# A branch that is not taken, between two quads of experts instead of behind the last

## The chip, the cores and the metric

The kernel runs on one core of a Trainium2 chip. The metric is the device time of one execution in microseconds (us), as the median of the runs. Five engines have a program each: TensorE (PE), VectorE (DVE), ScalarE (ACT), GpSimd (POOL) and SyncE (SP), which here only starts DMA transfers. They meet through semaphores.

## The reference, cut to what matters

Two layers over 256 tokens of width 1024, all in float32. In each layer comes attention of one kind or another, and then a mixture of experts in 4 groups of 8. A token picks one group, and in it two experts:

```python
for l in range(DEPTH):                                   # 2
    mod = c_act @ mod_w[l] + mod_b[l]
    ...
    x = x + gate1 * mix                                  # attention
    h = rms_norm(x, norm2_g[l]) * (1.0 + scale2) + shift2
    x = x + gate2 * hier_moe(h, ...)
# hier_moe, for each group g of 4, each expert e of 8:
hid = silu(hf @ w1[g, e]) * (hf @ w3[g, e])              # 1024 -> 512
y = y + (hid * gate[:, g, e]) @ w2[g, e]                 # 512 -> 1024
```

The weights of the 32 experts of a layer are read from memory whole: 3 x 2 MB each, 192 MB a layer.

## The kernel before

**Experts by quads.** The 32 experts are worked on as `QUADS` = 8 quads of four. An expert has 32 seats; the tokens that chose it are numbered (`m.rank`), and those with numbers 1 to 32 sit in the first round. For a quad, TensorE gathers the seated tokens of four experts by products with a 0/1 matrix `m.sel` (L772), VectorE and ScalarE scale and shift them into `m.seated` (L1538 and L953, the helper that records every activation), TensorE makes the two hidden products with four experts side by side (L788, four blocks of 32 products), VectorE multiplies them (L1542), TensorE turns the result (L800), makes the output products (L813, two blocks), VectorE applies the gate of the residual (L1549), and TensorE spreads the rows back over the tokens and adds them to banks 4 to 7 (L823). At the end of a quad VectorE makes `m.sel` for the next one (L1524); at its start it makes `m.sel_gate` (L1533). On each engine the eight quads are one hardware loop (`Fori`).

**Weights by a ring.** Every weight passes through `m.ring`, six slots of 2 MB (one unit each). A quad is 12 units, two to a block of L788 or L813. SP issues the units in the order of use (L323 for dense weights, L335 for experts) and waits before each until `m.ring_used`, which TensorE raises as it finishes a unit, has freed its slot. The next layer's dense units follow the eighth quad in the same ring. Its first four are the modulation weights, called F0 to F3 here: TensorE multiplies F0, F1 and F2 (L511), then turns the normed tokens (L540), then multiplies F3.

**Further rounds.** More than 32 tokens may choose an expert. The routing counts them and writes a row of flags, `m.over_i` (semaphore `over_ready`); flag 1 says that some expert has more than 32. Behind the loop over the quads each of PE, ACT, DVE and SP loads the flag into a register and branches:

```python
        pe.wait_ge(s["over_ready"], l + 1)
        with pe.If(pe.value_load(m.over_i[0:1, 1:2]) > 0):
            with pe.Fori(1, ROUNDS) as r:
                with pe.Fori(0, QUADS) as quad:
```

The body is another copy of the quad's code, run seven times over all eight quads with the next 32 seats each time and its own semaphores (`m.moe[l, "more"]`), and with weights loaded again. With the flag at 0 it is jumped over. Behind it TensorE makes one small product into bank 7 (L846), which only signals `end`; VectorE then copies the four banks to `m.x` (L1566; in the last layer ScalarE copies two of them, L1176), and the norm of the next layer or the output transfer (L357) follows.

Of the kernel before, what the change touches and what calls it, by code (L numbers as in the profile page):

```python
# [87 lines left out]
LAYER_UNITS = DENSE_UNITS + QUAD_UNITS * QUADS  # L88
ATT = P + T
# [208 lines left out]
def program_sync(sp, m, a, out):  # L298
# [18 lines left out]
    for l in range(DEPTH):  # L317
# [13 lines left out]
        with sp.Fori(0, QUADS) as quad:  # L331
            for u in range(QUAD_UNITS):
                g = g0 + u
                sp.wait_ge(m.ring_used, g - RING + 1 + QUAD_UNITS * quad)
                sp.dma_start(slot_pair(m, slot_of(g)), expert_unit(m, a, l, quad, u)).then_inc(  # L335
                    m.ring_full[slot_of(g)], 16)

        s = m.moe[l, "more"]
        sp.wait_ge(m.s["over_ready"], l + 1)
        with sp.If(sp.value_load(m.over_i[0:1, 1:2]) > 0):  # L340
            sp.wait_ge(m.ring_used, g0 + QUAD_UNITS * QUADS)
            with sp.Fori(1, ROUNDS) as r:
                with sp.Fori(0, QUADS) as quad:
# [7 lines left out]
                    sp.sem_inc(s["quads"], 1)  # L351
    rows = out.rearrange("b (t p) d -> p (b t) d", p=P)
# [138 lines left out]
def program_tensor(pe, m):  # L491
# [334 lines left out]
    def experts(l):  # L826
# [4 lines left out]
        with pe.Fori(0, QUADS) as quad:  # L831
            def landed(u):
                pe.wait_ge(m.ring_full[slot_of(g0 + u)], fills(g0 + u) + 32 * quad)
            quad_of_experts(e, quad, quad + 1, [slot_of(g0 + u) for u in range(QUAD_UNITS)], landed, m.ring_used)
        e = m.moe[l, "more"]
        pe.wait_ge(s["over_ready"], l + 1)
        with pe.If(pe.value_load(m.over_i[0:1, 1:2]) > 0):
            with pe.Fori(1, ROUNDS) as r:
                with pe.Fori(0, QUADS) as quad:
# [5 lines left out]

        pe.matmul(bank[7][0:1, 0:P], m.above[:, 0:1], m.ident[:, :], start=False, stop=True,  # L846
                  skip_group_check=True).then_inc(m.moe[l, "end"], 1)
# [100 lines left out]
def program_scalar(act, m, a):  # L948
# [186 lines left out]
    def experts(l):  # L1135
        with act.Fori(0, QUADS) as quad:
            quad_of_experts(l, "first", quad)
        act.wait_ge(s["over_ready"], l + 1)
        with act.If(act.value_load(m.over_i[0:1, 1:2]) > 0):
            with act.Fori(1, ROUNDS) as r:  # L1140
                with act.Fori(0, QUADS) as quad:
                    quad_of_experts(l, "more", (r - 1) * QUADS + quad)

# [53 lines left out]
def program_vector(dve, m):  # L1197
# [355 lines left out]
    def experts(l):  # L1553
        dve.wait_ge(s["row_ready"], 4 * (l + 1))
        with dve.Fori(0, QUADS) as quad:
            quad_of_experts(l, "first", quad, quad, quad + 1, m.iota[:, 0:SEATS])
        with dve.If(dve.value_load(m.over_i[0:1, 1:2]) > 0):
            with dve.Fori(1, ROUNDS) as r:
                seats = m.iota[:, bass.ds(SEATS * r, SEATS)]
                seat_tokens(m.moe[l, "more"], slice(0, 4), seats)  # L1560
                with dve.Fori(0, QUADS) as quad:
                    quad_of_experts(l, "more", (r - 1) * QUADS + quad, quad, (r - 1) * (QUADS + 1) + quad + 1, seats)
        dve.wait_ge(m.moe[l, "end"], 1)
# [93 lines left out]
```

## Time and profile before

| | |
|---|---|
| median of 3 runs | 1378.91 us (1375.66 to 1379.0) |
| the profiled execution, its own time | 1371.47 us |
| its span, first to last instruction | 1369.7 us |
| TensorE busy | 989.0 us (72%) |
| VectorE busy | 262.8 us (19%) |
| ScalarE busy | 213.9 us (16%) |
| mean granted TensorE clock | 0.868 of full speed |
| DMA | 489.78 MB, mean 358 GB/s over the span |

The profile is of one execution; times in it are microseconds from its first instruction. "Busy" leaves out register loads, branches and waits, so that these show only as idle time of their engine, with "issue" as the releaser when nothing else is seen to end it. SPq is the instruction queue of SP, PEld the weight loads of TensorE.

### The profile page before, as it was taken

What the parts mean: (1) busy time and instruction counts of PE and PEld (TensorE: products, weight loads), DVE (VectorE), ACT (ScalarE), POOL (GpSimd) and SP (SyncE); (2) the same over time, 40 slices, a digit from 0 to 9 for tenths busy, and PEclk for the clock granted to TensorE, in tenths of its full rate; (3) what the DMA queues carried; (4) which work ended last, traced back from release to release, by engine and by line L of the source; (5) the groups of instructions that cost most, each with busy time, mean ns of one, the idle gap of its engine ahead of it and who ended that gap; (6) DMA issues with size and microseconds to landing.
All of it is one profiled execution on the core that took longest, in us unless ns stands there. A gap on an engine that the chain in (4) does not pass through costs nothing.

```text
span 1369.7 us, 13973 instructions
## 1 busy us (share of the span) xinstructions
PE 989.0 (72%) x5668; PEld 443.5 (32%) x5668; DVE 262.8 (19%) x573; ACT 213.9 (16%) x431; POOL 30.4 (2%) x89
## 2 busy tenths in 40 slices
PE   4999898667565766766679999967476675757665
PEld 1445555222121222222146665532121231212121
DVE  0545534101000010100020366410000010000101
ACT  2223314001000000100010353410000010000000
POOL 3000000000000000000000022000000000000000
PEclk9999999788887888888789999999887888878787
DMA  9973716999999999999999336569999999999995
GB/s 355 392 224 123 307 62 278 423 422 422 423 421 422 422 423 422 421 422 423 422 405 376 136 117 253 235 277 422 423 422 423 422 422 422 422 422 422 422 422 216
DMA packets 90826, 489.78 MB, mean 358 GB/s; under 512 B 18208, under 2 KB 18336, under 8 KB 37544
## 3 DMA queue, kind: packets, MB, share of 16 engines
q1 hardware_dynamic: 87776, 487.95, 87.4%
q10 hardware_dynamic: 3016, 1.37, 0.4%
q8 instruction: 22, 0.36, 0.1%
q14 instruction: 12, 0.10, 0.0%
HBM read 488.25 MB, written 1.05 MB: 357 GB/s over the span
## 4 chain that ended last, share of the span: by engine, by line
DMA 53%; PE 39%; DVE 4%; issue 1%; ACT 1%; SPq 1%; DVEq 0%
DMA ring<-in_moe_w_dram 52%; PE bank L546 8%; PE bank L788 7%; PE bank L813 7%; PE bank L586 4%; PE bank L699 4%; PE bank L511 2%; DMA ring<-in_mod_w_dram 1%; PE bank L638 1%; SPq L335 1%; PE bank L540 1%; PE bank L654 1%; PE bank L749 1%; PE bank L823 1%; DVE tmp L1404 0%
## 5 line engine op out<-in xcount | busy, mean ns | idle before, releaser
L788 PE MATMUL bank<-ring,region 128*32 128x512 f32 x2048 | 303.9, 748 | 189.2 <-DMA ring<-in_moe_w_dram 187.5
L813 PE MATMUL bank<-ring,region 128*32 128x512 f32 x1024 | 168.5, 818 | 122.9 <-DMA ring<-in_moe_w_dram 122.9
L788 PEld LDWEIGHTS bank<-ring,region 128*32 128x32 f32 x2048 | 83.6, 133 | 396.1 <-issue 394.4
L813 PEld LDWEIGHTS bank<-ring,region 128*32 128x32 f32 x1024 | 46.0, 143 | 232.7 <-issue 232.7
L546 PE MATMUL bank<-ring,hT 128*128 128x512 f32 x256 | 115.4, 602 | 2.7 <-ACT hT L953 2.7
L1542 DVE TENSOR_TENSOR region<-region,bank 128x512 f32<-128x512 f32 x16 | 11.0, 688 | 497.6 <-PE bank L788 497.6
L953 ACT ACTIVATE region<-bank,shift,scale 128x128 f32<-128x128 f32 x64 | 24.1, 457 | 353.2 <-PE bank L772 353.2
L1549 DVE TENSOR_TENSOR region<-bank,region 128x512 f32<-128x512 f32 x32 | 20.6, 686 | 281.1 <-PE bank L813 281.1
L823 PE MATMUL bank<-region 128*128 128x512 f32 x128 | 59.2, 605 | 13.4 <-DVE region L1549 13.4
L546 PEld LDWEIGHTS bank<-ring,hT 128*128 128x128 f32 x256 | 47.9, 193 | 59.4 <-issue 56.7
L511 PE MATMUL bank<-ring,c_wide 128*32 128x512 f32 x384 | 52.0, 670 | 18.0 <-DMA ring<-in_mod_w_dram 18.0
L772 PEld LDWEIGHTS bank<-region,h 128*128 128x128 f32 x512 | 59.5, 192 | 7.7 <-issue 6.7
L586 PE MATMUL bank<-hT,ring 128*128 128x256 f32 x256 | 59.4, 392 | 2.7 <-ACT hT L953 2.7
L772 PE MATMUL bank<-region,h 128*128 128x128 f32 x512 | 60.0, 275 | 0.8 <-DVE region L1524 0.8
L1132 ACT COPY region<-bank 128x256 f32<-128x256 f32 x16 | 6.0, 372 | 349.2 <-PE bank L800 349.2
L699 PE MATMUL bank<-ring,hT 128*128 128x512 f32 x128 | 57.3, 598 | 0.4 <-issue 0.3
L586 PEld LDWEIGHTS bank<-hT,ring 128*128 128x128 f32 x256 | 49.8, 197 | 11.6 <-ACT hT L953 2.7
L953 ACT ACT_TABLE_LOAD x34 | 43.6, 1283 | 4.3 <-issue 3.7
L823 PEld LDWEIGHTS bank<-region 128*128 128x128 f32 x128 | 23.0, 189 | 52.0 <-DVE region L1549 29.0
L1538 DVE TENSOR_SCALAR region<-bank,scale,shift 128x128 f32<-128x128 f32 x64 | 21.9, 404 | 57.0 <-PE bank L772 57.0
L420 POOL TENSOR_TENSOR pr<-pr,strict 128x384 f32<-128x384 f32 x16 | 18.1, 1129 | 659.9 <-ACT pr L953 659.9
L699 PEld LDWEIGHTS bank<-ring,hT 128*128 128x128 f32 x128 | 23.5, 190 | 26.7 <-issue 26.7
(217 smaller groups left out, 649.7 us busy)
## 6 DMA issues: line engine op xcount, KB each, us to landing
ring<-in_moe_w_dram SPq DMA_DIRECT2D x192, 2048.0 KB, 20.9
ring<-in_mod_w_dram SPq DMA_DIRECT2D x24, 2048.0 KB, 12.3
ring<-in_ev_w_in_dram SPq DMA_DIRECT2D x6, 2048.0 KB, 22.0
ring<-in_od_w_in_dram SPq DMA_DIRECT2D x6, 2048.0 KB, 19.2
ring<-in_ev_w_out_dram SPq DMA_DIRECT2D x2, 2048.0 KB, 7.6
ring<-in_od_w_out_dram SPq DMA_DIRECT2D x2, 2048.0 KB, 8.1
x<-in_x_dram ACTq DMA_DIRECT2D x1, 1024.0 KB, 5.1
out_dram<-x SPq DMA_DIRECT2D x4, 256.0 KB, 2.5
```

Of the source, the lines that this page charges most:

```text
L420: pool.tensor_tensor(m.pr[hh % 2][:, :], m.pr[hh % 2][:, :], m.strict[:, :], ALU.mult).then_inc(m.s["sb_masked"], 1)
L511: last = pe.matmul(out[32 * j:32 * j + 32, :], m.c_wide[:, k, :], w[:, k - rows * e, i * COL:(i + 1) * COL], start=first, stop=end, skip_g ...
L546: last = pe.matmul(bank[b][:, 0:cols], m.hT[:, k, t * P:(t + 1) * P], w[:, k, :], start=(k == 0), stop=(k == KC - 1))
L586: last = pe.matmul(bank[proj_bank(i)][:, c * T:(c + 1) * T], w[:, k, lo:lo + P], m.hT[:, k, :], start=(k == 0), stop=(k == KC - 1))
L699: last = pe.matmul(bank[out_bank(half, i)][:, :], m.hT[:, 4 * half + k, t * P:(t + 1) * P], w[:, k, u * COL:(u + 1) * COL], start=(k == 0) ...
L772: last = pe.matmul(bank[2 + k // 4][:, (k % 4) * P:(k % 4 + 1) * P], m.h[:, t, k * P:(k + 1) * P], m.sel[:, t, :], start=(t == 0), stop=(t ...
L788: last = pe.matmul(bank[which][32 * j:32 * j + 32, :], m.seated[:, 4 * part + k, 32 * j:32 * j + 32], w, start=(part == 0 and k == 0), sto ...
L813: last = pe.matmul(bank[half][32 * j:32 * j + 32, :], m.hidT[:, 2 * part + c, 32 * j:32 * j + 32], w, start=(part == 0 and c == 0), stop=( ...
L823: pe.matmul(bank[4 + 2 * half + t][:, :], m.back[:, t, :], m.y_seat[:, half * COL:(half + 1) * COL], start=False, stop=False, skip_group_c ...
L953: return act.activation(out, in_, f, **kw)
L1538: ts(m.seated[:, k, :], bank[2][:, k * P:(k + 1) * P], m.scale[:, k:k + 1], m.shift[:, k:k + 1], ALU.mult, ALU.add).then_inc(e["seated_dve ...
L1549: tt(m.y_seat[:, cols], bank[half][:, :], m.gate2[:, cols], ALU.mult).then_inc(e["y_copied"], 1)
```

## The change

On PE, ACT, DVE and SP the loop over eight quads is split into one over `FIRST_QUADS` = 6 and one over the last two, both with the same body, and the wait for `over_ready`, the load of the flag and the branch over the further rounds stand between the two. TensorE's closing product L846 stays behind the last quad. So each engine's program has one more copy of the quad's code in each layer. Inside the branch there are new waits, so that the tiles which the rounds share with the first round are free, and VectorE makes the seventh quad's `m.sel` again before it leaves the branch. GpSimd has no part in it.

```diff
@@ -86,6 +86,7 @@
 O_OUT_AT = (15, 14)
 QUAD_UNITS = 12
 LAYER_UNITS = DENSE_UNITS + QUAD_UNITS * QUADS
+FIRST_QUADS = QUADS - 2
 ATT = P + T
 SCALE = HD ** -0.5
 EPS = 1e-6
@@ -328,17 +329,21 @@
                     load_mod_cols(sp, m, a, layer, group, m.got["late_cols"])
                 router_loads(sp, m, a)
         g0 += DENSE_UNITS
-        with sp.Fori(0, QUADS) as quad:
+
+        def quad_loads(quad):
             for u in range(QUAD_UNITS):
                 g = g0 + u
                 sp.wait_ge(m.ring_used, g - RING + 1 + QUAD_UNITS * quad)
                 sp.dma_start(slot_pair(m, slot_of(g)), expert_unit(m, a, l, quad, u)).then_inc(
                     m.ring_full[slot_of(g)], 16)
 
+        with sp.Fori(0, FIRST_QUADS) as quad:
+            quad_loads(quad)
+
         s = m.moe[l, "more"]
         sp.wait_ge(m.s["over_ready"], l + 1)
         with sp.If(sp.value_load(m.over_i[0:1, 1:2]) > 0):
-            sp.wait_ge(m.ring_used, g0 + QUAD_UNITS * QUADS)
+            sp.wait_ge(m.ring_used, g0 + QUAD_UNITS * FIRST_QUADS)
             with sp.Fori(1, ROUNDS) as r:
                 with sp.Fori(0, QUADS) as quad:
                     n = (r - 1) * QUADS + quad
@@ -349,6 +354,8 @@
                             s[f"full{u % RING}"], 16)
                     sp.wait_ge(s["used"], QUAD_UNITS * (n + 1))
                     sp.sem_inc(s["quads"], 1)
+        with sp.Fori(FIRST_QUADS, QUADS) as quad:
+            quad_loads(quad)
     rows = out.rearrange("b (t p) d -> p (b t) d", p=P)
     for i in range(OUT_UNITS * TT):
         half, t = divmod(i, TT)
@@ -828,10 +835,21 @@
         e = m.moe[l, "first"]
         pe.wait_ge(s["row_ready"], 4 * (l + 1))
         pe.wait_ge(s["h_chunked"], TT * (l + 1))
-        with pe.Fori(0, QUADS) as quad:
+
+        def first_round(quad):
             def landed(u):
                 pe.wait_ge(m.ring_full[slot_of(g0 + u)], fills(g0 + u) + 32 * quad)
             quad_of_experts(e, quad, quad + 1, [slot_of(g0 + u) for u in range(QUAD_UNITS)], landed, m.ring_used)
+
+        with pe.Fori(0, FIRST_QUADS) as quad:
+            first_round(quad)
+        further_rounds(l)
+        with pe.Fori(FIRST_QUADS, QUADS) as quad:
+            first_round(quad)
+        pe.matmul(bank[7][0:1, 0:P], m.above[:, 0:1], m.ident[:, :], start=False, stop=True,
+                  skip_group_check=True).then_inc(m.moe[l, "end"], 1)
+
+    def further_rounds(l):
         e = m.moe[l, "more"]
         pe.wait_ge(s["over_ready"], l + 1)
         with pe.If(pe.value_load(m.over_i[0:1, 1:2]) > 0):
@@ -842,9 +860,7 @@
                     def landed_more(u):
                         pe.wait_ge(e[f"full{u % RING}"], 32 * n + (16 if u < RING else 32))
                     quad_of_experts(e, n, (r - 1) * (QUADS + 1) + quad + 1, [u % RING for u in range(QUAD_UNITS)], landed_more, e["used"])
-
-        pe.matmul(bank[7][0:1, 0:P], m.above[:, 0:1], m.ident[:, :], start=False, stop=True,
-                  skip_group_check=True).then_inc(m.moe[l, "end"], 1)
+            pe.wait_ge(e["sel_made"], (ROUNDS - 1) * (QUADS + 1) + 1)
 
     pe.wait_ge(s["consts"], CONSTS)
     pe.wait_ge(s["c_ready"], 1)
@@ -1133,13 +1149,15 @@
             e["turned_copied"], 1)
 
     def experts(l):
-        with act.Fori(0, QUADS) as quad:
+        with act.Fori(0, FIRST_QUADS) as quad:
             quad_of_experts(l, "first", quad)
         act.wait_ge(s["over_ready"], l + 1)
         with act.If(act.value_load(m.over_i[0:1, 1:2]) > 0):
             with act.Fori(1, ROUNDS) as r:
                 with act.Fori(0, QUADS) as quad:
                     quad_of_experts(l, "more", (r - 1) * QUADS + quad)
+        with act.Fori(FIRST_QUADS, QUADS) as quad:
+            quad_of_experts(l, "first", quad)
 
     first_loads(act, m, a)
     act.wait_ge(m.got["c"], 16)
@@ -1552,14 +1570,20 @@
 
     def experts(l):
         dve.wait_ge(s["row_ready"], 4 * (l + 1))
-        with dve.Fori(0, QUADS) as quad:
+        with dve.Fori(0, FIRST_QUADS) as quad:
             quad_of_experts(l, "first", quad, quad, quad + 1, m.iota[:, 0:SEATS])
         with dve.If(dve.value_load(m.over_i[0:1, 1:2]) > 0):
+            dve.wait_ge(m.moe[l, "first"]["sel_made"], FIRST_QUADS + 1)
             with dve.Fori(1, ROUNDS) as r:
                 seats = m.iota[:, bass.ds(SEATS * r, SEATS)]
                 seat_tokens(m.moe[l, "more"], slice(0, 4), seats)
                 with dve.Fori(0, QUADS) as quad:
                     quad_of_experts(l, "more", (r - 1) * QUADS + quad, quad, (r - 1) * (QUADS + 1) + quad + 1, seats)
+                dve.wait_ge(m.moe[l, "more"]["sel_made"], (QUADS + 1) * r)
+            seat_tokens(m.moe[l, "more"], slice(4 * FIRST_QUADS, 4 * FIRST_QUADS + 4), m.iota[:, 0:SEATS])
+            dve.wait_ge(m.moe[l, "more"]["sel_made"], (ROUNDS - 1) * (QUADS + 1) + 1)
+        with dve.Fori(FIRST_QUADS, QUADS) as quad:
+            quad_of_experts(l, "first", quad, quad, quad + 1, m.iota[:, 0:SEATS])
         dve.wait_ge(m.moe[l, "end"], 1)
         for t in range(TT if l + 1 < DEPTH else 1):
             for half in range(OUT_UNITS):
```

## Rows read from the trace of the kernel before

**Rows 1.** The page, the chain of work that ended last, shares of the span by engine:
```profile
DMA 53%; PE 39%; DVE 4%; issue 1%; ACT 1%; SPq 1%; DVEq 0%
```

**Rows 2.** The page, DMA issues: KB each, median us to landing:
```profile
ring<-in_moe_w_dram SPq DMA_DIRECT2D x192, 2048.0 KB, 20.9
```

**Rows 3.** The chain of waits, 640 to 760: start, length, what:
```profile
681.53 0.14 issue
...
687.64 3.70 PE bank L823 x8
691.34 3.73 issue
...
710.64 16.43 PE bank L586 x64
...
728.93 14.01 PE bank L586 x64
```

**Rows 4.** Timeline, all engines, end of layer 1: start, length, in brackets idle before, releaser:
```profile
1363.82 0.38 PE L846 MATMUL bank<-ident,above 128*1 128x128 f32 x2 [0.88 <-issue]
...
1364.23 1.29 DVE L1566 COPY x<-bank 128x512 f32<-128x512 f32 x2 [4.12 <-PE bank L846]
```

**Rows 5.** The page, DMA queues: packets, MB, share of 16 engines:
```profile
q8 instruction: 22, 0.36, 0.1%
```

**Rows 6.** Timeline of TensorE, sixth to seventh quad, layer 0:
```profile
568.25 3.70 PE L823 MATMUL bank<-region 128*128 128x512 f32 x8 [0.84 <-DVE region L1549]
571.79 3.73 PE L772 MATMUL bank<-region,h 128*128 128x128 f32 x32
575.45 3.64 PE L788 MATMUL bank<-ring,region 128*32 128x512 f32 x32
582.25 5.34 PE L788 MATMUL bank<-ring,region 128*32 128x512 f32 x32 [3.15 <-DMA ring<-in_moe_w_dram]
```

**Rows 7.** Issues of line 323 (dense weights), 668 to 669, 676 to 679, 686 to 687.2:
```profile
L323 SPq DMA_DIRECT2D ring<-in_mod_w_dram x2: 382/422/461, 668.3 to 668.8; - x2
...
DMA to landing us min/median/max: 18.2/20.4/22.7
...
L323 SPq DMA_DIRECT2D ring<-in_mod_w_dram x2: 368/419/470, 676.7 to 677.2; - x2
...
DMA to landing us min/median/max: 19.7/22.1/24.5
...
L323 SPq DMA_DIRECT2D ring<-in_od_w_in_dram x1: 592/592/592, 686.8 to 686.8; - x1
...
DMA to landing us min/median/max: 20.2/20.2/20.2
```

**Rows 8.** Windows: stretch, us, busy (instructions) by engine, granted clock, DMA share, GB/s:
```profile
230.00:690.00 460.00, 297.59 (x1846) 107.48 (x1839) 36.56 (x75) 37.55 (x59) 0.00 (x0) 0.82 1.01 420
...
695.07:698.00 2.93, 2.93 (x17) 1.47 (x21) 2.24 (x4) 0.86 (x1) 0.00 (x0) 0.50 0.97 405
```

**Rows 9.** Timeline, all engines, start of layer 1:
```profile
700.49 1.15 ACT L953 ACTIVATE h<-x,rstd 128x1024 f32<-128x1024 f32 x1
...
702.16 2.06 PE L540 MATMUL bank<-ident,h 128*128 128x128 f32 x16
...
704.15 1.92 PE L511 MATMUL bank<-ring,c_wide 128*32 128x512 f32 x16
```

**Rows 10.** Timeline of TensorE, the same place in layer 1:
```profile
1253.12 3.64 PE L788 MATMUL bank<-ring,region 128*32 128x512 f32 x32 [2.37 <-DMA ring<-in_moe_w_dram]
```

**Rows 11.** Timeline of VectorE, sixth to seventh quad, layer 0:
```profile
573.78 1.37 DVE L1538 TENSOR_SCALAR region<-bank,scale,shift 128x128 f32<-128x128 f32 x4 [4.08 <-PE bank L772]
```

**Rows 12.** Issues of line 335, 562 to 571, then 576 to 582, with landing:
```profile
L335 SPq DMA_DIRECT2D ring<-in_moe_w_dram x2: 372/372/373, 567.4 to 568.0; - x2
...
L335 SPq DMA_DIRECT2D ring<-in_moe_w_dram x2: 373/373/373, 579.1 to 579.7; - x2
...
DMA to landing us min/median/max: 17.9/20.1/22.3
```

## The prediction

> **What bounds the kernel now.** I read the page's chain of the work that ended last first. DMA holds 53% of it and TensorE 39% [rows 1], so time saved on an engine counts only where the engine, and not a weight transfer, is last. The page's list of DMA issues then shows 192 transfers of expert weights [rows 2]. Eight quads of 12 units in two layers are 2 x 8 x 12 = 192: no quad is run a second time, so the branch for further rounds is passed over in both layers, and only the cost of passing over it is moved.
>
> Where is that cost? The chain in order of time shows the end of layer 0's experts [rows 3]. The last weights land at 681.53, L813 consumes them, L1549 on VectorE moves the result, the L823 products end at 691.34, and then TensorE stands for 3.73 us in "issue": it waits for no engine and no transfer. What lies there in its program is the loop's exit, the wait for `over_ready` (done since the first quad), the load of the flag, the branch, and a jump over the body of the further rounds to L846. At the end of layer 1 the same place costs 0.88 us on the last stretch to the output [rows 4]. So the removable time is at most 3.73 + 0.88 = 4.61 us, 0.33% of 1378.91.
>
> The difference of the two stalls tells what they are. The instructions are the same; at the end of layer 0 the next layer's weights fill the DMA queues, at the end of layer 1 nothing is left to load. The page has a queue of kind "instruction" with 22 packets and 0.36 MB, 16 KB each [rows 5]: program text comes by the same DMA engines. I read 0.88 us as flag, branch and a fetch with idle engines, and the other 2.85 us as the same fetch behind weight packets. The Trainium skill ("Runtime: NRT & Kernel Launch", Instruction fetch mechanics) says it likewise: text comes in 16 KB blocks, prefetch is only sequential, and a taken branch beyond the window waits for its target's block. The page's packet size agrees; the trace does not show to which jump a packet belongs.
>
> **Part 1: what is removed.** Layer 1: L846 follows the last L823 with no jump between. Inside the loop, from quad to quad, the L772 products start as L823 ends (568.25 + 3.70 = 571.95 against 571.79) [rows 6], so the nearest row prices a loop's turn at nothing. I take the whole 0.88 us, with 0 as the other end. VectorE's and ScalarE's own flag and branch leave this place too, but both were waiting for L846 already (VectorE for 4.12 us [rows 4]).
>
> Layer 0: 3.73 us go, but I must ask what is late next. L846 is followed by the modulation products of the next layer, L511, over four weight units F0 to F3, the transposes L540 standing before F3. SP issued F0 and F1 at 668.3 and 668.8, F2 and F3 at 676.7 and 677.2, and the times to landing [rows 7] give arrivals at 668.3 + 18.2 = 686.5, 668.8 + 22.7 = 691.5, 676.7 + 19.7 = 696.4 and 677.2 + 24.5 = 701.7: one unit in 5 us, since DMA has been full for the whole expert stage (share 1.01 from 230 to 690) [rows 8]. That flow does not move with this change. Today TensorE starts F3 at 704.15 [rows 9], 2.3 us after its arrival (701.7 + 0.14 from landing to start, as before L813 [rows 3]). With the stall gone, L846 ends near 691.7; F0 and F1 are there; F2 starts by 696.5 at the earliest and takes 1.9 us; the transposes need the second tile of h, ready at 700.49 + 1.15 - 3.73 = 697.9, and end 2.06 us after F2's end, near 700.5. Then F3 waits until 701.84. So of 3.73 us only 704.15 - 701.84 = 2.3 us get through, and up to 1.4 us of a remaining stall would cost nothing. Behind F3 the chain runs through L1236, L522 and the modulation to L586 at 710.64 with every later weight in time: the first of them was issued at 686.8 and landed after 20.2 us, at 707.0 [rows 7], ahead of 708.3. Layer 1's attention and routing hang on TensorE, VectorE and ScalarE, so 2.3 us carry through to its first quad, and from there to the end.
>
> **Part 2: what is put between quads six and seven.** The wait, the flag, the branch and the jump now stand between L823 and L772 on TensorE, between L1524 and L1533 on VectorE, behind the table load after L1132 on ScalarE, and between two pairs of weight issues on SP. DMA is full here too, so I price TensorE's stall at 3.73 us (ends: 0.88 with idle DMA, and 3 x 3.73 = 11.2 if the second loop's text comes on demand in three pieces and not one; the nearest row, the one jump under full DMA, had one stall). Queued behind it are the gather L772 and the first L788 block; the seventh quad's weights for that block are there. L772 would start at 575.5 in place of 571.79 and the block would end at 579.09 + 3.73 = 582.8. The next one waits for DMA until 582.25 today, 3.15 us of cover [rows 6], 2.37 in layer 1 [rows 10]. It starts 0.6 to 1.4 us late and ends far ahead of the block behind it, which waits for two more units, some 10 us of flow. Cost on the chain: 0. VectorE waits 4.08 us for the gather before L1538 [rows 11]; its own jump overlaps TensorE's, and only its excess over that would add to a cover as wide.
>
> SP: its jump lies between a pair issued at 567.4 and 568.0 and the next at 579.1 [rows 12], in 10.7 us of waiting. If TensorE is 3.7 us late, the pair of 579.1 goes out at 582.8. That pair's first unit lands 17.9 us after issue [rows 12] though one unit takes 5: some 12.9 us of queued work are ahead of it. The flow of weights does not notice. Without that cover, each microsecond would cost one, in both layers. The new end of the second loop costs SP what a loop's turn costs.
>
> **Sum.** 2.3 + 0.88 - 0 = 3.2 us. Against the profiled execution's 1371.47 that is 1368.3. The median of the runs shown is 1378.91, 7.4 us above the profile; both terms sit at layer ends and not in the DMA-bound length, so I take them as they are: 1378.91 - 3.2 = 1375.7.
>
> **TensorE's clock** is the unknown with a size. Right after the stall the granted clock is 0.50, the 1.2 GHz level [rows 8], after 3.73 us of idleness; later the first 64 L586 products take 16.43 us and the next 64 take 14.01 [rows 3]. Without the stall F0 may run at 2.4 GHz, which F3's arrival swallows; but new short waits before F2 and F3 may shift the low stretch. I put +-2.4 us on it, centre 0.
>
> **The rivals.**
> A, all of it comes through (the flow is earlier against TensorE than in the profile, or the clock gives some back): 4.6 us, 1374.3, with the clock 1372. For it: the profile is one execution. Against: F3's arrival is fixed to the last expert unit by four units of 5 us, 20.2 us, whereas TensorE without the stall would need only 704.15 - 3.73 - 681.53 = 18.9. Chance 0.2.
> B, the stall stays at L846: it belongs to the loop's exit into text that was never read, and the jump itself is cheap. Then nothing is gained, 1378.9, while the jump is hidden. For it: both ends of a layer have unread text behind the loop. Against: behind L846 the text is as unread, and L540 and L511 follow each other there with no gap [rows 9], and the page's packets are too few to be re-read at each turn. Chance 0.13. The Trainium skill has a rule for either side ("Advanced Engine Details and Errata", Control Flow Timing): a compare-and-branch is given at about 108 ns, which alone would make the moved part worth 0.2 us in both layers; the 3.73 us in the trace speak for the fetch, not for the branch.
> C, slower: the second loop, entered by a jump with DMA full, has its text fetched in pieces on TensorE or SP, and the ring's supply breaks. It decides from 12.9 us of delay to TensorE at the pair of 579.1, or 10.7 + 12.9 = 23.6 us on SP. At 20 us on TensorE it would cost 7 a layer: 1375.7 + 14 = 1390. For it: text nobody has timed. Against: the only measured jump under full DMA took 3.73. Chance 0.05.
> The rest, 0.62, is my forecast.
>
> **Range and chances.** The forecast's own range is 1375.7 +- 2.4 for the clock and some 1.5 for the median of three runs, which lay within 3.3 us. With A below and B above I give 1371.5 to 1380.5. A measurement of this kernel can hardly tell 0.3%, 4.1 us, from no change: my 3.2 lies inside, A just outside. Faster by more than 0.3%: 0.23 (A, and the forecast with the clock's help). Slower: 0.07 (C, and B with the clock against it). Within: 0.70.
>
> **What would show it.** In the changed profile: "issue" before L846 near 0 in both layers; a wait of 3 to 4 us before L772 of the seventh quad in both layers; the L788 block behind it still starting at a weight landing or under 1.5 us later; F3's L511 with a DMA wait ahead of it of 1 to 1.5 us, where there is none now; DMA share unchanged at full through the expert stages. I am wrong if L846 still has its gap (B), if F3 starts without a wait (A), or if a slice of the expert stage shows less than full DMA (C).

## The result

Over 10 executions of each kernel the changed one took 1368.58 us and the one before 1375.9 us: a ratio of 0.9948, with a 95% interval of 0.9931 to 0.9965, 7.2 us or 0.5% faster (4.8 to 9.5 us). I had forecast 1375.7 us within 1371.5 to 1380.5, with 0.70 on a time within 0.3% of the kernel before. The measured time lies 2.9 us below the range. The two profiles show that what moved is what I had said; how much it is worth, and against which median, is where I was off. The ratios below leave out one execution of the kernel with two jumps, which took 1511.72 us at a granted clock of 0.667.

The chain of waits of the changed kernel (start, length, what) answers to [rows 3]:

```profile
575.88 4.07 issue
...
681.09 23.93 DMA ring<-in_mod_w_dram
...
705.07 1.97 PE bank L518 x16
```

The stall has moved: 4.07 us of "issue" now stand in front of the seventh quad's gather, and the chain in layer 0's end goes through a weight transfer (681.09 + 23.93) into L518, the new line of L511. That transfer is F3. The timeline around it (start, busy, in brackets idle before and releaser) answers to [rows 9] and [rows 3]:

```profile
685.27 5.34 PE L820 MATMUL bank<-ring,region 128*32 128x512 f32 x32 [4.60 <-DMA ring<-in_moe_w_dram]
...
691.43 3.70 PE L830 MATMUL bank<-region 128*128 128x512 f32 x8 [0.83 <-DVE region L1567]
...
695.06 0.27 PE L849 MATMUL bank<-ident,above 128*1 128x128 f32 x1
...
700.08 1.92 PE L518 MATMUL bank<-ring,c_wide 128*32 128x512 f32 x16 [1.20 <-DMA ring<-in_mod_w_dram]
...
705.07 1.92 PE L518 MATMUL bank<-ring,c_wide 128*32 128x512 f32 x16 [1.09 <-DMA ring<-in_mod_w_dram]
...
711.56 3.76 PE L593 MATMUL bank<-hT,ring 128*128 128x256 f32 x8 [2.65 <-ACT hT L969]
```

L849, the closing product, starts as L830 (L823 before) ends, with nothing in brackets. F2 waits 1.20 us for its weights and F3 1.09 us; before, neither waited. The end of layer 1 looks the same, against [rows 4]:

```profile
1360.30 3.70 PE L830 MATMUL bank<-region 128*128 128x512 f32 x8 [0.84 <-DVE region L1567]
...
1363.93 0.38 PE L849 MATMUL bank<-ident,above 128*1 128x128 f32 x2
...
1364.35 1.29 DVE L1590 COPY x<-bank 128x512 f32<-128x512 f32 x2 [3.17 <-PE bank L849]
```

The 0.88 us are gone. The place between the sixth and the seventh quad, TensorE's timeline in layer 0 and in layer 1, and then SP's issues and their landing (580 to 590), against [rows 6, 10, 12]:

```profile
572.17 3.70 PE L830 MATMUL bank<-region 128*128 128x512 f32 x8 [0.83 <-DVE region L1567]
579.95 5.40 PE L779 MATMUL bank<-region,h 128*128 128x128 f32 x32 [4.07 <-issue]
585.28 7.07 PE L795 MATMUL bank<-ring,region 128*32 128x512 f32 x64
595.81 5.34 PE L795 MATMUL bank<-ring,region 128*32 128x512 f32 x32 [3.46 <-DMA ring<-in_moe_w_dram]
```

```profile
1248.18 4.90 PE L779 MATMUL bank<-region,h 128*128 128x128 f32 x27 [3.81 <-issue]
1253.69 0.72 PE L779 MATMUL bank<-region,h 128*128 128x128 f32 x5 [0.61 <-issue]
1254.34 7.07 PE L795 MATMUL bank<-ring,region 128*32 128x512 f32 x64
```

```profile
L337 SPq DMA_DIRECT2D ring<-in_moe_w_dram x2: 373/373/373, 588.9 to 589.5; - x2
...
DMA to landing us min/median/max: 11.7/13.9/16.1
```

The stall is 4.07 and 3.81 us, and more than I had priced comes behind it: the gather takes 5.40 us where it took 3.73, and in layer 1 it stops once more for 0.61 us in its middle. The windows of the gather in layer 0, before and changed (stretch, us, busy time of PE, PEld, DVE, ACT and POOL, granted clock, DMA share, GB/s), show why it is slower:

```profile
571.79:575.52 3.73, 3.73 (x37) 3.61 (x39) 1.37 (x4) 0.00 (x0) 0.00 (x0) 1.00 1.01 422
```

```profile
579.95:585.35 5.40, 5.40 (x36) 5.28 (x40) 1.37 (x4) 0.00 (x0) 0.00 (x0) 0.69 1.01 419
```

After 4.07 us of idleness the granted clock is at 0.50, the 1.2 GHz level, for the first 3.4 us of the gather, and 5.40 x 0.69 = 3.73: the clock is the whole of the difference. The first L795 block ended, and the next pair of weight units was issued, at 588.9. Without the stall the gather would have started at 575.7 and the block ended 7.3 us later (571.79 to 579.1 in [rows 6, 12]), at 583.0, so SP was 5.9 us late and not 3.7. The second L795 block followed at once, 2.7 us later against the L823 or L830 products than before (588.9 - 572.17 against 582.25 - 568.25), where I had allowed 1.4. The issued unit landed 11.7 us after its issue and not 17.9. DMA stayed full: the experts' stage kept its length to 0.3 us (see the table below), and the third block waits for its weights again (3.46 us; 4.61 before).

### The profile page after: what moved, and what is told of

Its sections match the earlier page's. It is cut to its first block, busy times and chain, and to the rows that moved or that the text cites. A ratio compares the mean times of both kernels' runs of the same rounds, so it can differ in the third digit from the quotient of the medians.

```text
span 1369.9 us, 13973 instructions
## 1 busy us (share of the span) xinstructions
PE 993.6 (73%) x5668; PEld 445.0 (32%) x5668; DVE 262.6 (19%) x573; ACT 203.5 (15%) x423; POOL 30.2 (2%) x89
## 4 chain that ended last, share of the span: by engine, by line
DMA 54%; PE 39%; DVE 3%; issue 1%; ACT 1%; SPq 1%; DVEq 0%
DMA ring<-in_moe_w_dram 50%; PE bank L553 9%; PE bank L795 7%; PE bank L820 7%; PE bank L593 4%; PE bank L706 4%; DMA ring<-in_mod_w_dram 3%; PE bank L518 2%; PE bank L645 1%; SPq L337 1%; PE bank L762 1%; PE bank L539 1%; PE bank L756 1%; PE bank L661 1%; PE bank L830 1%
## 5 line engine op out<-in xcount | busy, mean ns | idle before, releaser
L795 PE MATMUL bank<-ring,region 128*32 128x512 f32 x2048 | 298.3, 737 | 178.3 <-DMA ring<-in_moe_w_dram 176.6
L795 PEld LDWEIGHTS bank<-ring,region 128*32 128x32 f32 x2048 | 82.4, 131 | 380.9 <-issue 379.2
L553 PE MATMUL bank<-ring,hT 128*128 128x512 f32 x256 | 119.2, 618 | 2.6 <-ACT hT L969 2.6
L779 PE MATMUL bank<-region,h 128*128 128x128 f32 x512 | 63.5, 285 | 9.3 <-issue 8.5
L830 PE MATMUL bank<-region 128*128 128x512 f32 x128 | 59.2, 605 | 13.4 <-DVE region L1567 13.4
L779 PEld LDWEIGHTS bank<-region,h 128*128 128x128 f32 x512 | 62.6, 200 | 17.0 <-issue 16.0
L518 PE MATMUL bank<-ring,c_wide 128*32 128x512 f32 x384 | 52.3, 672 | 17.9 <-DMA ring<-in_mod_w_dram 17.9
L706 PE MATMUL bank<-ring,hT 128*128 128x512 f32 x128 | 57.3, 598 | 0.4 <-issue 0.3
L830 PEld LDWEIGHTS bank<-region 128*128 128x128 f32 x128 | 23.0, 189 | 51.6 <-DVE region L1567 28.7
L427 POOL TENSOR_TENSOR pr<-pr,strict 128x384 f32<-128x384 f32 x16 | 17.9, 1120 | 658.8 <-ACT pr L969 658.8
## 6 DMA issues: line engine op xcount, KB each, us to landing
ring<-in_mod_w_dram SPq DMA_DIRECT2D x24, 2048.0 KB, 12.4
```

What stands on the lines that cost most here:

```text
L427: pool.tensor_tensor(m.pr[hh % 2][:, :], m.pr[hh % 2][:, :], m.strict[:, :], ALU.mult).then_inc(m.s["sb_masked"], 1)
L518: last = pe.matmul(out[32 * j:32 * j + 32, :], m.c_wide[:, k, :], w[:, k - rows * e, i * COL:(i + 1) * COL], start=first, stop=end, skip_g ...
L553: last = pe.matmul(bank[b][:, 0:cols], m.hT[:, k, t * P:(t + 1) * P], w[:, k, :], start=(k == 0), stop=(k == KC - 1))
L706: last = pe.matmul(bank[out_bank(half, i)][:, :], m.hT[:, 4 * half + k, t * P:(t + 1) * P], w[:, k, u * COL:(u + 1) * COL], start=(k == 0) ...
L779: last = pe.matmul(bank[2 + k // 4][:, (k % 4) * P:(k % 4 + 1) * P], m.h[:, t, k * P:(k + 1) * P], m.sel[:, t, :], start=(t == 0), stop=(t ...
L795: last = pe.matmul(bank[which][32 * j:32 * j + 32, :], m.seated[:, 4 * part + k, 32 * j:32 * j + 32], w, start=(part == 0 and k == 0), sto ...
```

## Why the two profiled executions do not show the gain

The profiled executions took 1371.47 us before and 1371.6 us after. The gain is missing there, because the stretch ahead of the first quad, whose instructions the change does not touch, took 222.25 us in the one profile and 225.63 us in the other. Over all the profiles taken for this study that start lies between 220.30 and 227.57 us (but for the one kernel whose jump stands ahead of it). Some of it goes with TensorE's clock: the windows 23.4 to 60 us (the clock is the third number from the right) of the two kernels, and of one more execution of the kernel before:

```profile
23.40:60.00 36.60, 33.07 (x166) 16.80 (x167) 14.91 (x44) 7.72 (x17) 3.34 (x4) 0.87 1.05 390
```

```profile
23.40:60.00 36.60, 33.14 (x160) 16.55 (x152) 12.53 (x40) 7.21 (x15) 3.33 (x4) 0.81 1.04 389
```

```profile
23.40:60.00 36.60, 31.77 (x170) 16.05 (x167) 16.25 (x48) 7.72 (x17) 3.34 (x4) 0.95 1.05 390
```

The start is the shorter, the higher the clock: 222.25 us at 0.87, 225.63 at 0.81, 220.86 at 0.95. Whether that is all of it was not tested.

So I compare stretches that begin and end with the same event:

| profile | first gather starts | last L813 block to first projection, layer 0 | last L813 block to closing product, layer 1 | first gather to last L813 block, layers 0 / 1 |
|---|---|---|---|---|
| before | 222.25 | 28.97 | 11.36 | 459.4 / 459.4 |
| before, again | 220.86 | 29.22 | 11.62 | 459.5 / 459.4 |
| changed | 225.63 | 26.29 | 10.28 | 459.6 / 459.7 |
| changed, again | 223.61 | 26.28 | 10.48 | 459.6 / 459.3 |

Each entry is a difference of two start times in the timeline of TensorE (711.56 - 685.27 = 26.29 above). With the profiles of the next section the two layer ends are worth about 2.9 and 1.0 us, and the experts' stage costs 0 to 0.3 us a layer.

## The experiments

Ratios are against executions of the kernel before on the same chip. The stretches are those of the table above; "gap" is the issue time ahead of the closing product, and the packets are those of queue q8 [rows 5].

| run | ratio (95%) | gap, layers 0 / 1 | layer 0's end | layer 1's end | instruction packets |
|---|---|---|---|---|---|
| before, again | 0.9999 (0.9983 to 1.0016) | 4.12 / 1.13 | 29.22 | 11.62 | 22 |
| changed, again | 0.9974 (0.9954 to 0.9994) | none | 26.28 | 10.48 | 26 |
| no branch | 0.9953 (0.9938 to 0.9969) | none | 26.29 | 10.41 | 18 |
| split only | 1.0002 (0.9984 to 1.0021) | 4.15 / 0.93 | 29.64 | 11.30 | 26 |
| short body | 0.9954 (0.9935 to 0.9972) | none | 26.29 | 10.44 | 18 |
| TensorE only | 0.9960 (0.9940 to 0.9981) | none | 26.30 | 10.40 | 26 |
| all but TensorE | 0.9995 (0.9977 to 1.0012) | 3.81 / 0.94 | 29.02 | 11.36 | 22 |
| layer 0 only | 0.9971 (0.9951 to 0.9991) | none / 0.98 | 26.30 | 11.45 | 26 |
| ahead of the quads | 1.0084 (1.0056 to 1.0112) | none | 26.57 | 9.80 | 26 |
| two jumps | 1.0038 (1.0016 to 1.0060) | none | 26.28 | 9.80 | 30 |
| five jumps | 1.0307 (1.0273 to 1.0342) | none | 26.40 | 10.93 | 42 |

**The same kernels again.** The kernel before:

> The kernel before once more, as a control: ratio 1.000, and a second profile of it. Theory 1 (the change is worth 3.2 to 3.6 us, as the two profiles show by stretches, and the rest of the 7.3 us between the medians is spread between executions): issue before L846 again 3.7 us in layer 0 and 0.9 in layer 1. Theory 2 (the stall under full DMA is usually longer than in the one profile): 5 to 8 us in layer 0.

and the changed one:

> The changed kernel once more. Theory 1: 3 to 4 us faster, ratio 0.997 to 0.998. Theory 2: 0.995, as in the first comparison. In the profile, by both: from the last expert landing to the start of F3 19.9 us in layer 0, and no gap before L849.

The control gave 0.9999. The changed kernel gave 3.6 us (0.8 to 6.3) in this comparison where the first gave 7.2 (4.8 to 9.5). The stall of the kernel before was 4.12 us here, not 5 to 8, so theory 2, a stall that is usually much longer than in the profile, has no support: the longest of the four profiles with the jump in the old place has 4.15 us.

**No branch at all.** The edit, on TensorE (SP, ScalarE and VectorE alike):

```diff
-        e = m.moe[l, "more"]
-        pe.wait_ge(s["over_ready"], l + 1)
-        with pe.If(pe.value_load(m.over_i[0:1, 1:2]) > 0):
...
         pe.matmul(bank[7][0:1, 0:P], m.above[:, 0:1], m.ident[:, :], start=False, stop=True,
```

> The kernel before without the branch for further rounds: no wait for over_ready, no flag load, no branch, no body, on all four engines; the eight quads stay one loop. With these inputs no round is left out. If the whole worth of the change is the skipped jump at the two ends, this takes the same as the changed kernel (within 1 us), and its layer ends look the same: F3 behind a DMA wait, no gap before the closing product. If the change also gained by something in its loops (text laid out otherwise, eight fewer table loads on ScalarE), this stays behind the changed kernel by 2 to 4 us.

6.4 us faster (4.3 to 8.5), not to be told from the changed kernel, and the layer ends are those of the changed kernel to 0.1 us. Nothing that the change does beside clearing the two ends has to be assumed, and by the layer ends moving the branch brings all that deleting it would; the two totals, 3.6 and 6.4 us, are too uncertain to tell them apart.

**The loops split, the branch left behind.**

```diff
+PARTS_OF_QUADS = ((0, FIRST_QUADS), (FIRST_QUADS, QUADS))
...
-        with pe.Fori(0, QUADS) as quad:
-            def landed(u):
...
+        for lo, hi in PARTS_OF_QUADS:
+            with pe.Fori(lo, hi) as quad:
+                def landed(u):
```

> The kernel before with the loop over quads split into six and two on all four engines, but the branch still behind the last quad. If the jump at the layer ends is all: ratio 1.000, 3.7 and 0.9 us of issue before the closing product as before. If the split itself (layout of the text, table loads) gave the 4 us that my sum lacks: 0.997.

Ratio 1.0002, gap 4.15 us. The split by itself gives nothing that shows, although ScalarE's table loads (L953) fell from 34 to 26, as in the changed kernel.

**The branch kept in place, its body short.** This tells the jump from the branch:

```diff
         with pe.If(pe.value_load(m.over_i[0:1, 1:2]) > 0):
-            with pe.Fori(1, ROUNDS) as r:
...
+            pe.wait_ge(e["sel_made"], 1)
```

> The kernel before, the branch in its old place on all engines, but on TensorE the body of the branch is one wait and not the seven rounds (the further rounds are left out; with these inputs none is run). The wait for over_ready, the flag load and the branch itself stay. Theory 1, the stall is the fetch of the text behind a far jump: the issue before the closing product falls from 3.7-4.15 to under 1 us in layer 0 and from 0.9-1.1 to under 0.6 in layer 1, F3 gets its DMA wait, total 3 to 4 us shorter, as with the changed kernel. Rival, the stall is the flag load and the branch: the gaps stay, ratio 1.000.

The timeline of TensorE at layer 0's end, flag load and branch still between the first two of these rows, and the page's instruction queue (packets, MB, share) of the kernel with the short body and of the changed one:

```profile
690.98 3.70 PE L823 MATMUL bank<-region 128*128 128x512 f32 x8 [0.83 <-DVE region L1543]
694.61 0.27 PE L840 MATMUL bank<-ident,above 128*1 128x128 f32 x1
...
704.61 1.92 PE L511 MATMUL bank<-ring,c_wide 128*32 128x512 f32 x16 [1.06 <-DMA ring<-in_mod_w_dram]
```

```profile
q8 instruction: 18, 0.29, 0.1%
```

```profile
q8 instruction: 26, 0.43, 0.1%
```

With the body gone, wait, flag and branch leave no gap, in either layer, where I had left room for 1 and 0.6 us. So all of the 3.73 us, and all of the 0.88 us, go with the jump over the long body.

**The branch itself is in the trace**, as an instruction of TensorE's sequencer, which the view calls PEldq. The rows are the kernel before in layer 0 and in layer 1, and then the short body, both layers (duration in ns, smallest, median, largest; first and last start):

```profile
L837 PEldq COMPARE_BRANCH  x1: 5987/5987/5987, 689.0 to 689.0; - x1
L837 PEldq COMPARE_BRANCH  x1: 3310/3310/3310, 1360.5 to 1360.5; - x1
```

```profile
L837 PEldq COMPARE_BRANCH  x2: 208/209/210, 692.4 to 1361.0; - x2
```

The windows of the kernel before over these two branches, and the instruction queue in the same two stretches:

```profile
689.00:695.03 6.03, 2.34 (x6) 0.76 (x4) 0.00 (x0) 0.00 (x0) 0.00 (x0) 0.99 1.03 425
1360.50:1363.80 3.30, 2.44 (x6) 0.76 (x4) 0.00 (x0) 0.00 (x0) 0.00 (x0) 1.00 0.02 5
```

```profile
q8 instruction: 1, 0.02, 1.1%
```

```profile
q8 instruction: 1, 0.02, 1.8%
```

The sequencer is ahead of the products: it begins the branch 2.3 to 2.4 us before the last L823 product ends. The jump takes 5.99 us with DMA full and 3.31 us with DMA at 0.02, and the gaps of 3.73 and 0.88 us are only what sticks out behind the products. One 16 KB packet begins inside each branch: at 692.5, 3.5 us after the branch began, in layer 0, and at 1361.5, 1.0 us after it, in layer 1. From the packet's begin to the next product it is then much the same, 2.56 and 2.35 us. So the two jumps differ by how long the fetch takes to begin (2.5 of the 2.68 us), as a fetch queued behind weight packets would; [rows 3, 4] alone had made me take 0.88 us for a whole fetch. In the short body's trace no packet of q8 begins between 689 and 695. The other engines' jumps over their own bodies take 0.05 to 0.06 us in the kernel before.

This is the rule of the Trainium skill ("Runtime: NRT & Kernel Launch", Instruction fetch mechanics) that a taken branch beyond the text at hand waits for its target's block, and the trace agrees. For the branch alone the Trainium skill ("Advanced Engine Details and Errata", Control Flow Timing) gives about 108 ns for a compare-and-branch; TensorE's took 208 and 210 ns here with the short body, and VectorE's 63 ns.

The number of instruction packets fits: with the quads in one loop, 22 with the two jumps and 18 without; with the loop in two parts, 26 with two jumps and, below, 30 with four and 42 with ten. That is two packets of 16 KB for each jump with its body, and the other 4 of the 26 go with the two more copies of the loop. A body's own text is also up to 32 KB, an estimate from the copies of the loop (two copies, four packets), so the count alone would not tell a fetch of the skipped text from one of the text behind it; what holds TensorE is told by the times.

**Which engine.** The move on TensorE alone, with SP, ScalarE and VectorE as before, and the opposite:

> The move on TensorE alone; SP, ScalarE and VectorE branch behind the last quad as before (which works because no further round is run here). If TensorE's jump is all: as the changed kernel, 3.5 to 5 us faster, stall of 4 us before the gather of the seventh quad. If the other engines' part or ScalarE's eight fewer table loads give anything: less than the changed kernel by that.

> The move on SP, ScalarE and VectorE, TensorE branches behind the last quad as before. If TensorE's jump is all: ratio 1.000, gaps before the closing product of 3.7-4.15 and 0.9-1.1 us. Otherwise up to 1.5 us faster.

TensorE alone gives 0.9960; the other three together 0.9995. The change is one engine's jump. The packets of q8 go with TensorE as well: 26 in the first, 22 in the second. The two rows of TensorE that matter, the gather of the seventh quad in the first and the closing product in the second:

```profile
573.93 5.25 PE L773 MATMUL bank<-region,h 128*128 128x128 f32 x32 [3.89 <-issue]
```

```profile
694.03 0.37 PE L853 MATMUL bank<-ident,above 128*1 128x128 f32 x1 [3.81 <-issue]
```

**Which layer.** The move on TensorE in layer 0 alone:

> The move on TensorE alone and in layer 0 alone; in layer 1 TensorE branches behind the last quad as before. By the stretches of the profiles so far layer 0's end is worth 3.0 us (29.3 us from the last expert landing to the first projection, against 26.3) and layer 1's 1.0 us (11.4 against 10.4 us from the last landing to the closing product). So: 26.3 in layer 0, 11.4 with 0.9 to 1.1 us of issue in layer 1, and a total 3 to 4.5 us below the kernel before, one less than with both. If the time that the profiles lack sits in layer 1, the total is only 2 to 3 us below.

26.30 us at layer 0's end, 11.45 at layer 1's, where the row is

```profile
1364.74 0.38 PE L846 MATMUL bank<-ident,above 128*1 128x128 f32 x2 [0.98 <-issue]
```

and 4.0 us faster in total (1.2 to 6.7). By stretches it should be 2.9. Most of the gain is layer 0's, as in my sum.

**Is F3 what layer 1 waits for?** One more product ahead of the closing one, in layer 0 alone:

```diff
+        if l == 0:
+            pe.matmul(bank[2][:, :], m.back[:, 0, :], m.y_seat[:, 0:COL], start=True, stop=True)
         pe.matmul(bank[7][0:1, 0:P], m.above[:, 0:1], m.ident[:, :], start=False, stop=True,
```

> The changed kernel with one more product of 128 x 512 (0.93 us, into a bank whose contents nobody needs) ahead of the closing product of layer 0 alone. If F3's landing is what bounds the start of layer 1: F3 still starts 19.8 us after the last expert weights landed and the first projection 26.3 us after them, F3's DMA wait shrinks from 1.09 to 0.2 us. If not: both move by 0.9 us, to 20.7 and 27.2.

TensorE's timeline at layer 0's end in this kernel:

```profile
686.35 5.75 PE L820 MATMUL bank<-ring,region 128*32 128x512 f32 x32 [4.61 <-DMA ring<-in_moe_w_dram]
...
696.47 1.02 PE L850 MATMUL bank<-region 128*128 128x512 f32 x2
697.42 0.27 PE L851 MATMUL bank<-ident,above 128*1 128x128 f32 x1
...
706.14 1.92 PE L518 MATMUL bank<-ring,c_wide 128*32 128x512 f32 x16 [1.07 <-DMA ring<-in_mod_w_dram]
...
712.63 16.69 PE L593 MATMUL bank<-hT,ring 128*128 128x256 f32 x64 [2.65 <-ACT hT L971]
```

The closing product is 11.07 us behind the last expert block (697.42 - 686.35) where it was 9.79 (695.06 - 685.27), and still F3 starts 19.79 us behind it (19.80 in the changed kernel) and the projection 26.28 (26.29). The extra product is free. I had expected F3's own wait to shrink and it did not (1.07 us); F2's did, from 1.20 us to 0, so the later closing product was made up there. What bounds the start of layer 1 is F3's landing, and rival A's premise is wrong. (One execution, 1373.1 us, not timed against the others.)

**How wide is the cover?** TensorE's jump more than once in a row in the new place:

```diff
             first_round(quad)
-        further_rounds(l)
+        for _ in range(5):
+            further_rounds(l)
```

> The changed kernel with TensorE's flag load and branch over the further rounds five times in a row between the sixth and the seventh quad (none of the bodies is run). One jump made the pair of weight issues behind it 6.0 us late (588.9 for 582.9) and left a landing 11.7 us after issue; five should make it 6.0 + 4 x 3.9 = 21.6 us late. By my sum the flow of weights has 12.9 us of queued work there, so DMA runs dry for 21.6 - 12.9 = 8.7 us a layer: each expert stage 9 us longer, the whole 15 to 19 us longer than the changed kernel. If the cover is wider than that (later waits of TensorE make it up): under 5 us longer. If the jumps behind the first are cheap because the text was fetched already: no change.

TensorE's timeline behind the sixth quad, five jumps:

```profile
574.83 3.70 PE L830 MATMUL bank<-region 128*128 128x512 f32 x8 [0.84 <-DVE region L1568]
608.00 6.65 PE L779 MATMUL bank<-region,h 128*128 128x128 f32 x32 [29.47 <-issue]
614.58 10.51 PE L795 MATMUL bank<-ring,region 128*32 128x512 f32 x96
```

Windows of the same run: stretch, us, busy time of PE, PEld, DVE, ACT and POOL, granted clock, DMA share, GB/s:

```profile
600.00:620.00 20.00, 12.00 (x84) 8.19 (x88) 1.37 (x4) 1.51 (x4) 0.00 (x0) 0.65 0.06 10
620.00:640.00 20.00, 12.60 (x86) 3.64 (x78) 0.69 (x1) 0.60 (x1) 0.00 (x0) 0.74 1.00 417
```

Both of my numbers were too kind. Five jumps stand 29.47 us and not the 4.07 + 4 x 3.9 = 19.7 of my expectation: 6.35 us for each behind the first ((29.47 - 4.07) / 4). The gap of the first is cut by the products above it, that of the others is not. The branches themselves took 6.22, 7.01, 7.03, 4.81 and 4.80 us in layer 0. The second and the fourth:

```profile
L856 PEldq COMPARE_BRANCH  x1: 7005/7005/7005, 582.8 to 582.8; - x1
L856 PEldq COMPARE_BRANCH  x1: 4808/4808/4808, 597.7 to 597.7; - x1
```

The DMA share was 1.01 over the second and 0.05 over the fourth: the price of a jump falls as DMA runs dry, within one run. It did run dry, with 10 GB/s for 20 us. The first L795 block ended near 614.58 + 3.5 = 618.1 instead of 578.4 + 7.3 = 585.7 (3.5 us is a third of the 96 products), 32.4 us late. The stage from the first gather to the last expert block grew by 24.4 us (227.57 to 711.54, 484.0, against 459.6). The cover was 8.0 us. The whole took 42 us more than the kernel before, where I had expected 15 to 19 more than the changed one. With two jumps:

> The changed kernel with TensorE's flag load and branch twice in a row between the sixth and the seventh quad. Five in a row stood 29.5 us and lengthened layer 0's expert stage by 24.4: 6.4 us for each jump behind the first, and 8 to 10 us of cover in place of my 12.9. So two should make the pair of weight issues 6.0 + 6.4 = 12.4 us late and the stage 2.5 to 4.5 us longer, the whole 5 to 9 us longer than the changed kernel. If my 12.9 held: no change.

The same timeline with two:

```profile
570.66 3.70 PE L830 MATMUL bank<-region 128*128 128x512 f32 x8 [0.83 <-DVE region L1568]
586.08 6.79 PE L779 MATMUL bank<-region,h 128*128 128x128 f32 x32 [11.72 <-issue]
592.80 10.51 PE L795 MATMUL bank<-ring,region 128*32 128x512 f32 x96
```

The block ended near 596.3 instead of 574.2 + 7.3 = 581.5, 14.8 us late, and the stage grew by 6.0 us (223.86 to 689.50, 465.6, against 459.6): cover 8.8 us. I had expected 12.4 us late and 2.5 to 4.5 us of stage. In layer 1, by the issues of the same pair, the cover was 9.6 us with five jumps and 8.5 with two. The whole is 5 us slower than the kernel before. My 12.9 us came from the time to landing less one unit of 5 us. But the late pair's first unit landed 8.7 us after its issue with five jumps and 8.3 with two, on a queue that had run empty, and 17.9 - 8.7 = 9.2 is near the cover. So what I had left out is the time from an issue to its first data, which counts once the queue is empty. So the changed kernel, 5.9 us late, sits 2 to 3 us from the edge and not 9.

**Without cover.** TensorE's flag load and branch ahead of the first quad:

```diff
+        further_rounds(l)
         with pe.Fori(0, FIRST_QUADS) as quad:
             first_round(quad)
-        further_rounds(l)
```

> The changed kernel, but on TensorE the flag load and the branch stand ahead of the first quad, where no weight transfer is last and TensorE's work frees the ring. Theory (the move pays only because DMA covers the stall): the gather of the first quad, 0.40 us behind the seats now, waits for over_ready (2.4 us later) and then for flag, branch and text, 2 to 4 us more with little on the DMA queues; nothing takes that back, so 4 to 6.5 us a layer are lost against the changed kernel: 8 to 13 us slower than it, 4 to 9 us slower than the kernel before. Rival (the place does not matter, only the end of the layer has to be clean): as the changed kernel.

TensorE's timeline at the first gather of layer 0 in this kernel:

```profile
226.64 0.39 PE L770 MATMUL bank<-sent,ones 128*128 128x32 f32 x2
234.47 5.67 PE L779 MATMUL bank<-region,h 128*128 128x128 f32 x32 [7.44 <-issue]
```

11.5 us slower than the kernel before (7.7 to 15.4), and so some 15 to 19 us slower than the changed one, more than the 8 to 13 that I had allowed. The gap ahead of the gather is 7.44 us in layer 0 and 7.07 in layer 1, where it was 0.40, and the gather itself takes 5.67 in place of 3.84: 8.9 and 8.4 us a layer. Of the gap 2.4 us are the wait for `over_ready` (in the changed kernel the flags are written at 228.0 and the gather starts at 225.63); the other 4.6 are flag and jump. The two branches of this run, with a DMA share of 0.02 over both:

```profile
L855 PEldq COMPARE_BRANCH  x2: 3490/3550/3609, 230.5 to 906.9; - x2
```

They took as long as the one at the end of layer 1 before (3.31 us), but nothing ran above them. So the 0.88 us there were not the whole of a fetch with idle DMA, as I had read them.

## Why the prediction was off

**What moves and where it goes** was right: no further round is run; the stall leaves L846 in both layers (gap none, against [rows 3, 4]); it reappears ahead of the seventh quad's gather (4.07 and 3.81 us); the weights keep flowing; F3 becomes a wait of 1.09 us, forecast as 1 to 1.5; only TensorE counts. The reading of the stall was half right: the jump's fetch is the stall, and full DMA adds 2.68 us to it (I had 2.85), but "0.88 us as flag, branch and a fetch with idle engines" was wrong, for that jump takes 3.31 us, of which the products hid 2.4. The trace does show to which jump a packet belongs, by its time. On the new place's side the stall was priced near enough (3.73 for 4.07 and 3.81), the low clock behind it at nothing (1.67 us in the gather), and the 12.9 us of queued work were 8 to 10; that these cost nothing here was the width of the cover, not the sizes in my sum. Rival B fell with the short body and with the gaps; rival C's mechanism is real, shown with two and five jumps, but not reached by the change itself. Rival A's sum of 4.6 us lies nearer to the measured gain than my 3.2, by the wrong reason, for F3 does limit layer 0's end.

**Terms that were mis-sized.** "2.3 us get through" in layer 0 measured 2.9: of four ends with the stall in place the profile that I had was the shortest (28.97, 29.22, 29.64 and 29.02 us; mean 29.2), while the cleared end is 26.3 in all profiles but two (26.40 and 26.57), held by the landing. On that shortest profile it is 2.7: F3 started 19.80 us behind the last expert block and not 20.2, as I had from the times to landing. "0.88" in layer 1 measured 1.0 (11.4 against 10.4). The sum was 3.2 and by stretches it is 3.9.

**The step that failed** is "I take them as they are: 1378.91 - 3.2". The miss is 1375.7 - 1368.58 = 7.1 us, and it has three parts: 3.0 us of base, 0.7 us of mis-sized terms, and 3.4 us by which the first comparison lies above what the stretches give. The median of three executions stood 3.0 us above that of ten (1375.9), and sets of 33, 29 and 17 more gave 1374.7, 1375.3 and 1375.4 (one of 15 gave 1372.9). I had widened the range by 1.5 us for this; with 1375.2 in its place the same range would have been 1367.8 to 1376.8 and held 1368.58, with the gain still too small. The third part is the first comparison itself: 7.2 us against 3.6 for the same two kernels the second time.

**What stays open.** Five comparisons of kernels whose ends are clean in both layers (0.9948, 0.9974, 0.9953, 0.9954, 0.9960) have a mean of 0.9958, 5.8 us. The stretches account for 3.9. One part of the rest was seen: from the first projection of layer 1 to its first gather two profiles with clean ends took 180.32 and 181.62 us (no branch, TensorE only) where all four with the stall took 182.3 to 182.6. In those two the first 64 projection products took 15.50 and 15.75 us in place of 16.43, at a granted clock of 0.91 and 0.89 in place of 0.85, which was my "+-2.4 us". Over seven profiles with a clean end of layer 0 (without those of the jump ahead of the quads, twice and five times) that makes 0.4 us. The last 1.5 us I can't place; each comparison is uncertain by 2 us, and the runs don't tell chance from a cause.

## What to carry to other kernels

A guarded body that is never run is not free: the jump over a large one makes the engine wait for the text behind it, 3.3 to 3.6 us on TensorE with DMA idle and 5.9 to 6.4 with DMA full, of which work queued ahead can hide some 2.4. It should stand where the engine waits for DMA anyway, or have its body made short. Price such a place by two numbers, how late the engine gets in all (here 5.9 us for a stall of 4.07) and how late the next transfer may be issued before the queue is empty (8 to 10 us for six slots of 2 MB); by the second, a second jump in the same place turned the gain into a loss. Look at the branch instruction's own duration, and not only at the gap behind it. And when a change is worth a few thousandths, take the base from more than three executions and compare stretches between like events, since the untouched start of this program alone moved by 7 us between profiles.

## What the runs showed of the hardware

A loop's turn on TensorE shows no gap with a body of 238 products (counts of the page over 16 quads; 0 us, [rows 6]). One forward jump over one such body took 5.91 to 6.42 us as an instruction with DMA full (17 jumps in eleven profiles) and 3.31 to 3.61 us with DMA idle (seven jumps), in place of 0.21 us over a body of one wait. With DMA full 3.71 to 4.15 us of it show as idle time, where it is the only jump of its place; with DMA idle 0.88 to 1.13 us at the end of layer 1. Further jumps directly behind took 7.0 to 7.2 us each with DMA full and 4.4 to 4.8 with DMA run dry. Each jump with its body goes with two 16 KB packets, one of which begins inside the branch.

The gather behind the jump ran slow as well: 5.40 us for 3.73 in the changed kernel, and 5.67, 6.65 and 6.79 in the kernels with the jump ahead of the quads, five times and twice. In the changed kernel the granted clock, 0.50 after 4.07 us of idleness, accounts for all of it; in the kernel with two jumps the window ahead of and into the gather reads:

```profile
580.00:590.00 10.00, 3.92 (x18) 3.92 (x19) 0.10 (x1) 0.00 (x0) 0.00 (x0) 0.50 1.01 410
```
